# Recurrent pairs with all products as 64x64 quarters, in two row steps

## What is computed

```python
def wkv7_scan(r, w, k, v, kk, a, reverse):          # 8 heads of 64, per direction
    def step(state, inp):
        r_t, w_t, k_t, v_t, kk_t, a_t = inp
        sa = jnp.einsum('bhij,bhj->bhi', state, -kk_t)
        state = (state * w_t[:, :, None, :] + sa[..., None] * (kk_t * a_t)[:, :, None, :]
                 + v_t[..., None] * k_t[:, :, None, :])
        return state, jnp.einsum('bhij,bhj->bhi', state, r_t)
    ...
y = direction(0, False) + direction(1, True)
...
branch = jnp.einsum('bsnc,ncd->bsnd', ys, w_branch)  # three branches
gates = jax.nn.sigmoid(gl.reshape(b, s, N_BRANCH, D_MODEL) + b_gate)
merged = jnp.sum(gates * branch, axis=2)
```

## Time and profile before

| | |
|---|---|
| median of 3 runs | 2549.43 us (2548.84 to 2550.6) |
| the profiled execution | 2548.45 us |
| its span, first to last instruction | 2546.7 us |
| TensorE busy | 2484.2 us, 98% |
| VectorE, ScalarE, GpSimd busy | 1439.2, 527.6, 316.1 us |
| the pairs of layer 0, from the first scores to the mean (L972) | 194.96 to 353.67, 158.71 us |
| the pairs of layer 1 | 829.89 to 987.83, 157.94 us |

### The profile page before, as it was taken

The page is one execution under the profiler, slowest core; times in us unless marked ns, Lnnn a source line. Parts: engine busy times, 40 slices in busy tenths (PEclk is TensorE's granted clock), DMA queues, the critical chain, the costliest instruction groups (busy, mean ns, idle before and its releaser), DMA issues. The chain is left out here.

```text
span 2546.7 us, 38463 instructions
## 1 busy us (share of the span) xinstructions
PE 2484.2 (98%) x15968; PEld 1905.6 (75%) x15968; DVE 1439.2 (57%) x2688; ACT 527.6 (21%) x1249; POOL 316.1 (12%) x367
## 2 busy tenths in 40 slices
PE   8999999999999999999999999999999999999998
PEld 7887886854788788685477747888886666666997
DVE  1576655855157655573357735555334488854775
ACT  1342220100134222010014910000003243411000
POOL 2002102110100210221000000000000155410110
PEclk9999999999999999999999999999999999999999
DMA  7331125987433212598632022222222534334553
GB/s 269 116 116 63 57 81 170 303 292 256 147 116 117 68 52 84 179 306 289 239 125 67 2 66 71 96 83 75 91 87 69 165 101 135 121 102 146 167 173 107
DMA packets 253603, 341.80 MB, mean 134 GB/s; under 512 B 7252, under 2 KB 179412, under 8 KB 253304
## 3 DMA queue, kind: packets, MB, share of 16 engines
q1 hardware_dynamic: 241632, 311.71, 37.4%
q10 hardware_dynamic: 8920, 17.67, 2.1%
q0 software_dynamic: 2880, 9.96, 1.0%
HBM read 338.13 MB, written 1.19 MB: 133 GB/s over the span
## 5 line engine op out<-in xcount | busy, mean ns | idle before, releaser
L1058 PE MATMUL PS<-MEM 128*128 128x256 f32 (+1 forms) x2632 | 447.9, 332 | 2.6 <-ACT MEM L1515 1.2
L1058 PEld LDWEIGHTS PS<-MEM 128*128 128x128 f32 x2632 | 406.3, 190 | 43.8 <-issue 1.9
L416 PE MATMUL PS<-MEM 128*128 128x256 f32 x1632 | 356.0, 379 | 0.0
L1474 ACT ACTIVATE MEM<-PS 128x256 f32<-128x256 f32 (+4 forms) x405 | 162.0, 429 | 907.8 <-PE PS L416 221.1
L416 PEld LDWEIGHTS PS<-MEM 128*128 128x128 f32 x1632 | 308.6, 190 | 42.5 <-issue 1.3
L462 PE MATMUL PS<-MEM 128*128 128x512 f32 x608 | 265.4, 597 | 9.1 <-DMA MEM<-w_down 4.3
L2094 DVE SCALAR_TENSOR_TENSOR MEM<-MEM 128x512 f32<-128x512 f32 x280 | 214.4, 798 | 53.7 <-DMA MEM<-ada_w 48.0
L462 PEld LDWEIGHTS PS<-MEM 128*128 128x128 f32 x608 | 115.3, 191 | 155.3 <-issue 141.2
L3038 POOL TENSOR_TENSOR MEM<-MEM 128x1 f32<-128x1 f32 (+1 forms) x34 | 21.6, 637 | 1269.4 <-DVE MEM L2040 812.1
L696 PE MATMUL PS<-MEM 128*128 128x256 f32 x768 | 178.3, 384 | 0.0
L1371 PE MATMUL PS<-MEM 128*128 128x512 f32 (+1 forms) x512 | 171.5, 488 | 0.0
(11 more groups left out here) (384 smaller groups left out, 3259.8 us busy)
## 6 DMA issues: line engine op xcount, KB each, us to landing
MEM<-w_in SPq DMA_DIRECT2D x54, 1024.0 KB, 5.4
MEM<-ada_w SPq DMA_DIRECT2D x48, 1024.0 KB, 7.5
MEM<-w_up SPq DMA_DIRECT2D x32, 1024.0 KB, 5.4
MEM<-w_down SPq DMA_DIRECT2D x32, 1024.0 KB, 5.1
MEM<-ssm_w_in SPq DMA_DIRECT2D x24, 1024.0 KB, 5.4
MEM<-ffn_gate SPq DMA_DIRECT2D x22, 1024.0 KB, 5.3
MEM<-ffn_up SPq DMA_DIRECT2D x22, 1024.0 KB, 5.4
MEM<-ffn_down SPq DMA_DIRECT2D x20, 1024.0 KB, 5.1
```

What stands on the lines that cost most here:

```text
L416: ins = pe.matmul(bank[:, 0:T], W[:, k, c * P:(c + 1) * P], XT[:, k, :], start=k == 0, stop=k == KT - 1)
L1058: ins = pe.matmul(out, left[:, k, :], right[:, k, :], start=k == 0, stop=k == 3)
L1474: act.activation(out, view(b), func, **kw).then_inc(S("bank_read_by_act"), 1)
```

## The change

All products between the first scores and the end of the pairs become 64x64 quarters, apart from the transposes of the keys. Scores are split into two column halves. Two tiles are now summed together: in a first turn the upper 64 rows of one tile's contraction and the lower 64 of the other, each in two column halves, and in a second turn the other rows, behind a wait (`half_summed`) on the end of the first turn. One step is one contraction slice of both tiles in one turn, so a pair of tiles has as many steps as two tiles had. A slot ends when tiles end; steps left over are owed to the next slot. The slots' numbers are new.

Right side, solve and outputs take both groups of the pair together. Each is cut in two row steps: one with the 64 rows of each group that feed both column halves, the other with the rest, without the zero quarter; between them stands a wait (`row_step`) on the end of the first. The right side of both groups now has its first step after `level_xt` of level 3 and its second after `level_z` of level 4, and one bank per group instead of two. `solve_first` comes ahead of the slot XO, `solve_second` and `outputs_first` behind it, `outputs_second` and `outputs_third` behind the slot sa. ScalarE copies both right sides at level 4; VectorE reads the states of both groups ahead of the results.

```diff
--- before.py
+++ after.py
@@ -57,10 +57,10 @@
-FILL_SLOT = {"mask": (4, 0, 0, 0), "begin": (10, 0, 0, 0),
- ("z", 1): (2, 4, 4, 4), ("z", 2): (0, 0, 0, 0), ("z", 3): (0, 0, 0, 0), ("z", 4): (0, 0, 0, 0), ("z", 5): (4, 4, 4, 4),
- ("x", 1): (0, 0, 0, 0), ("x", 2): (0, 4, 4, 0), ("x", 3): (0, 0, 0, 0), ("x", 4): (0, 4, 4, 4), ("x", 5): (4, 4, 4, 4),
- "W": (4, 4, 4, 4), "XO": (2, 2, 2, 4), "sa": (2, 4, 4, 4)}
+FILL_SLOT = {"mask": (4, 0, 0, 0), "begin": (14, 0, 0, 0),
+ ("z", 1): (2, 2, 2, 2), ("z", 2): (0, 0, 2, 2), ("z", 3): (2, 2, 2, 2), ("z", 4): (2, 2, 2, 2), ("z", 5): (0, 2, 2, 4),
+ ("x", 1): (0, 0, 2, 0), ("x", 2): (0, 2, 2, 0), ("x", 3): (0, 0, 0, 2), ("x", 4): (0, 2, 2, 2), ("x", 5): (2, 2, 2, 4),
+ "W": (4, 4, 4, 4), "XO": (0, 2, 2, 4), "sa": (2, 4, 4, 4)}
@@ -427,7 +427,16 @@
-used = [0]
+used, halves, row_steps = [0], [0], [0]
+def rows_stepped(ins):
+    ins.then_inc(S("row_step"), 1)
+    row_steps[0] += 1
+def other_rows():
+    pe.wait_ge(S("row_step"), row_steps[0])
@@ -678,46 +687,61 @@
-    n_tiles = [0]
-    def open_tile(key):
-        n_tiles[0] += 1
-        return bank_for(key, None if spin[1] == NBANK else NBANK - 2 + n_tiles[0] % 2)
+    def pair_of_tiles(keys, by, W, c, src, nk):
+        if spin[1] == NBANK:
...
+            return
+        banks = [bank_for(key, NBANK - 2 + j) for j, key in enumerate(keys)]
+        for turn in range(2):
+            if turn:
+                pe.wait_ge(S("half_summed"), halves[0])
+            for k in range(nk):
+                for j, b in enumerate(banks):
+                    r = HB * (j ^ turn)
+                    for o in (0, HB):
+                        ins = pe.matmul(PS[o:o + HB, b, 0:T], W[r:r + HB, k, (c + j) * P + o:(c + j) * P + o + HB], src[r:r + HB, k, :],
+                                        start=turn == 0 and k == 0, stop=turn == 1 and k == nk - 1)
+                    if turn == 0 and k == nk - 1:
+                        ins.then_inc(S("half_summed"), 1)
+                        halves[0] += 1
+                    if turn == 1 and k == nk - 1:
+                        numbered(keys[j], by, b)
+                        done(ins)
+                if turn == 0 or k < nk - 1:
+                    yield 0
+        yield 2
     def gate_tiles(n):
         for s in range(4):
             W = a_slab(w_in[l], O_G + D * n + 256 * s)
-            for c in range(2):
...
+            work = pair_of_tiles([("gl", l, n, 2 * s + c) for c in range(2)], "act", W, 0, XT, KT)
+            yield from shut(work, 2)
     def branch_tiles(n, Y):
         for s in range(2):
             W = b_slab(w_branch[l, n], 0, 512 * s)
-            for c in range(4):
...
+            yield from pair_of_tiles([("br", l, n, 4 * s + c) for c in range(2)], "dve", W, 0, Y, 4)
+            work = pair_of_tiles([("br", l, n, 4 * s + c) for c in (2, 3)], "dve", W, 2, Y, 4)
+            yield from shut(work, 2)
+    def shut(work, tiles):
...
@@ -735,9 +759,16 @@
+    owed = [0]
     def slot(pair, name):
-        tiles_in[l, pair, name] = sum(next(gate_run) for _ in range(FILL_SLOT[name][pair]))
+        owed[0] += FILL_SLOT[name][pair]
+        tiles = 0
+        while owed[0] and not tiles:
+            tiles += next(gate_run)
+            owed[0] -= 1
+        tiles_in[l, pair, name] = tiles
@@ -784,7 +815,8 @@
             for half in range(2):
                 i, ct, pb, h = inst[2 * j + half]
                 rhs = KR[pb:pb + 64, d, ct, c, :, :].rearrange("p a b -> p (a b)")
-                ins = pe.matmul(banks[half][:, 256 * j:256 * j + 256], BK[pb:pb + 64, d, ct, c, part, :], rhs, start=True, stop=True)
+                for o in (0, HB):
+                    ins = pe.matmul(banks[half][o:o + HB, 256 * j:256 * j + 256], BK[pb:pb + 64, d, ct, c, part, o:o + HB], rhs, start=True, stop=True)
                 if j == 1:
                     done(ins)
@@ -871,55 +903,145 @@
                 if i == 3:
                     done(ins)
-    def right_side(g):
...
+    opened = {}
+    def open_banks(name, gs):
+        for g in gs:
+            opened[name, g] = bank_for((name, l, g))
+    def right_first(gs):
+        for g in gs:
+            emptied(pe, ("sk", l, g, 1))
+            if g >= 4:
+                emptied(pe, ("st", l, g - 4))
+        open_banks("rh", gs)
+        for i in range(4):
+            for g in gs:
+                d, c, wave, inst = instances(g)
+                _, ct, pb, h = inst[i]
+                f, b = HB * d, opened["rh", g]
+                to = [PS[o:o + HB, b, i * HB:(i + 1) * HB] for o in (0, HB)]
+                for j in range(2):
+                    ins = pe.matmul(to[j], AK[g % 2][f:f + HB, i, HB * j:HB * j + HB], VTK[f:f + HB, c, 64 * h:64 * h + 64],
+                                    start=i == 0, stop=wave == 0 and i == 3 and j == d)
...
+                if i == 3:
+                    rows_stepped(ins)
+    def right_second(gs):
+        other_rows()
+        for i in range(4):
+            for g in gs:
+                d, c, wave, inst = instances(g)
+                _, ct, pb, h = inst[i]
+                r, b = HB - HB * d, opened["rh", g]
+                to = [PS[o:o + HB, b, i * HB:(i + 1) * HB] for o in (0, HB)]
+                ins = pe.matmul(to[1 - d], AK[g % 2][r:r + HB, i, r:r + HB], VTK[r:r + HB, c, 64 * h:64 * h + 64],
+                                start=False, stop=i == 3 and (wave == 0 or pb != r))
...
+                if i == 3:
+                    numbered(("rh", l, g), "act", b)
                     done(ins)
-    def solve(g):
-        i2 = g % 2
-        emptied(pe, ("XO", l, g))
-        emptied(pe, ("rh", l, g, 1))
-        bank = take(("sa", l, g), "act")
+    def solve_first(gs):
+        for g in gs:
+            emptied(pe, ("rh", l, g))
+        open_banks("sa", gs)
         for i in range(4):
-            ins = pe.matmul(bank[:, i * 64:(i + 1) * 64], AB[g % 4][:, i, 0:P], RH[i2][:, i, :], start=True, stop=True)
...
+            for g in gs:
+                for o in (0, HB):
+                    ins = pe.matmul(PS[o:o + HB, opened["sa", g], i * HB:(i + 1) * HB], AB[g % 4][o:o + HB, i, o:o + HB], RH[g % 2][o:o + HB, i, :],
+                                    start=i == 0, stop=i == 3 and o == HB * (g % 2))
+                if i == 3:
+                    rows_stepped(ins)
+    def solve_second(gs):
+        for g in gs:
+            emptied(pe, ("XO", l, g))
+        other_rows()
+        for i in range(4):
+            for g in gs:
+                f = HB * (g % 2)
+                r, b = HB - f, opened["sa", g]
+                ins = pe.matmul(PS[r:r + HB, b, i * HB:(i + 1) * HB], AB[g % 4][f:f + HB, i, r:r + HB], RH[g % 2][f:f + HB, i, :],
+                                start=False, stop=i == 3)
+                if i == 3:
+                    numbered(("sa", l, g), "act", b)
+                    done(ins)
+    def outputs_first(gs):
...
+                to = PS[pb:pb + HB, opened["y", g], (i // 2) * P:(i // 2 + 1) * P]
+                pe.matmul(to, VTK[f:f + HB, c, 64 * h:64 * h + 64], AK[g % 2][f:f + HB, i, P:2 * P], start=i < 2, stop=False)
+                if wave and pb == f:
+                    pe.matmul(to, ST[pb:pb + 64, d, ct, :], KR[pb:pb + 64, d, ct, c, 1, :], start=False, stop=False)
+    def outputs_second(gs):
+        for g in gs:
+            emptied(pe, ("sa", l, g))
+        if gs[0] < 4:
+            open_banks("st", gs)
+        for i in range(4):
+            for g in gs:
+                d, c, wave, inst = instances(g)
+                _, ct, pb, h = inst[i]
+                f = HB * d
+                if wave == 0:
+                    to = PS[pb:pb + 64, opened["st", g], (i // 2) * 64:(i // 2) * 64 + 64]
+                    pe.matmul(to, BKT[g % 2][f:f + HB, 2 * (i // 2), pb:pb + 64], SA[g % 2][f:f + HB, i, :], start=i < 2, stop=False)
...
+                to = PS[pb:pb + HB, opened["y", g], (i // 2) * P:(i // 2 + 1) * P]
+                ins = pe.matmul(to, SA[g % 2][f:f + HB, i, :], AB[g % 4][f:f + HB, i, P:2 * P], start=False, stop=False)
+                if i == 3:
+                    rows_stepped(ins)
+    def outputs_third(gs):
+        other_rows()
...
+                ins = pe.matmul(PS[pb:pb + HB, b, o + r:o + r + HB], SA[g % 2][r:r + HB, i, :], AB[g % 4][r:r + HB, i, P + r:P + r + HB], start=False, stop=False)
+                ins = pe.matmul(PS[pb:pb + HB, b, o + r:o + r + HB], VTK[r:r + HB, c, 64 * h:64 * h + 64], AK[g % 2][r:r + HB, i, P + r:P + r + HB],
+                                start=False, stop=i >= 2 and not (wave and pb == r))
+                if wave and pb == r:
+                    ins = pe.matmul(PS[pb:pb + HB, b, o:o + P], ST[pb:pb + 64, d, ct, :], KR[pb:pb + 64, d, ct, c, 1, :], start=False, stop=i >= 2)
+                if i == 3:
+                    numbered(("y", l, g), "dve", b)
+                    done(ins)
     spin[:] = [0, NBANK - 2]
     for g in (0, 1):
@@ -936,8 +1058,8 @@
             if m == 2 and pair < 2:
```

(55 more changed lines are left out.)

94 lines of the change are left out of this document (45 added, 49 removed).

## The result

The changed kernel takes 2561.16 us (median of 4 runs, 2559.32 to 2563.61) for 2549.14 of the kernel before: 1.0047 times as long, 95% interval 1.0030 to 1.0065. The prediction was 2522.

A forecast was written before the change was run, and what follows sets the result against it. TensorE, busy 98% of the span, was taken as the bound. Per layer, work 122.2 + added waits 2.8 + front 3.8 + clock 1.6 + stalls 14.1 = 144.5 us, against 316.65 for both: 2522 median, 8-in-10 range 2497 to 2546.

The forecast's parts named there:

- Rival (1): Quarter passes over 256 columns don't run four quadrants at a time: 197 us per layer, 2626 us total; chance 0.07.
- The front: TensorE's idle time before the first level product of each layer's stage, 3.8 us per layer with 0.3 before the flips.
- chain: TensorE's stalls behind ScalarE's copies and VectorE's masks in the recurrent pairs: 14.1 us per layer, bounds half and double.
- Rival (2): Stalls on ScalarE and VectorE in the pairs take the whole gain back: 28 us instead of 14, total 2549; chance 0.10.
- Outputs: TensorE's work on the output products of the four pairs: 8.2 us per layer.
- levels: TensorE's work on the level products, 1856 passes at 14.9 ns: 27.7 us per layer.
- tiles: TensorE's work on the tiles, 960 quarter passes at 54.4 ns over 256 columns: 52.2 us per layer.
- rival (5): Instruction issue paces each quarter pass over 256 columns at 60 ns: 6.8 us more per layer, 2535 us; chance 0.01.
- The added waits: Also called own waits: half_summed and row_step waits in the stage, 7 x 0.4 = 2.8 us per layer.
- The clock: A stretch at granted clock 0.50 behind the idle time before the first level product: 1.6 us per layer.
- Drains: Time lost whenever TensorE leaves 64*64 passes for another split: 0.30 us each, about 48 per layer, some 14 us.
- Rival (4): Gaps between blocks come from waits, not the split, so 48 x 0.30 us stay: 2541 us; chance 0.05.

## Why the prediction was wrong

- **What held.** Quarters over 256 columns run four at a time: 32 passes from 195.75 to 197.48 in the kernel after, and 54.4 ns in the row measured alone. Rival (1) is out. The front came out at 4.1 for 3.8, with a stretch at 0.50 there, as said. The sum of work, own waits and chain was near, 139.1 for 141.7 and 139.0. Rival (2), the chain that takes it all back, is out as well: the chain's named waits are 3.2 us in layer 0, not 28.
- **That sum held by luck: two errors cancel.** The starts of consecutive passes in layer 0, less the waits that the trace names, add up to 142.1 us of work, 138.7 without the half-rate loss, where I had 122.2 and 2.8 of own waits. Outputs took 12.6 for 8.2, levels 33.2 for 27.7, tiles 59.8 for 52.2 (the half-rate time, mostly in the tiles, included). The paces were taken from blocks in full stream; that blocks which begin and end more often don't reach them is my reading, which no run tests. The chain's named waits were 3.2, where I had 12.6 without the branch tiles: the longer work and the stalls, as far as can be told, covered the rest.
- **The step that failed most**, by the trace's sums, is issue: the sum has no term for it, and rival (5), "Issue becomes the bound", got a chance of 0.01. Of the 16.7 and 20.6 us by which the stages exceed 144.5, the stalls without a releaser are 7.2 and 12.4. I priced issue as a pace per pass, and the trace did refuse that: 16 ns a pass runs. The limit is another: how fast the program arrives. 4209 passes for 2881 are 34 packets of instructions for 23 in each stage, and wherever 128 passes run in under some 3.5 us, TensorE stands for the rest. The 62 ns per matmul that the Trainium skill, "TensorE: Matmul & The Clock Gate", section "Wait — 56ns, not 53.3ns?", gives for one decode setting did not describe it: between the stalls passes over 64 columns run at 16 ns and passes over 256 columns at 54.4. (The prediction charged it to the passes over 256 columns alone; on the narrow ones it would have been far more.) The rows to see it by were in the trace of before, as the queue of instructions with its 16 KB packets, and as one wait of 0.35 us without a releaser; the prediction uses neither.
- **The added waits** are the other step that failed. I looked at the semaphores, between the turns of a pair and between row steps, priced those at 2.8, and missed that a pair takes both tile banks at once, so that a tile now waits for VectorE's reading of two: 4.8 and 3.5 us. I had only a neighbour of it, two branch tiles that reach VectorE in one slot of the last pair, 1.5. By the runs this step weighs most: with 14 of the 20 tiles whole, the waits of the tiles and at the front fall from 16.5 us in both layers to 1.6, the half-rate loss from 9.5 to 1.7, the stalls without a releaser only from 19.6 to 18.4, and the time goes from 2561 to 2543. No run takes these stalls away alone.
- **The clock** cost 3.4 and 6.1 us for 1.6: beyond the front, stretches at half rate stood at two waits of 0.92 and 1.32 us close together, at a stall of 1.60 without a releaser, and at one tile's wait of 1.86.
- **Drains.** That leaving 64*64 costs 0.30 us was neither shown nor refuted as such. Rival (4) was not needed: the run with whole tiles in small slots, which keeps these drains, is as fast as any here.
- **Outside the stages** 2.9 us were lost, 3.3 of them between the layers, where TensorE waits 1.6 us for w_up and 1.5 for w_down at once (before 0.5 at the most). I had written that nothing moves on SP's queue. No run took this apart; it stays open.

## What to carry to other kernels

Count TensorE's instructions before cutting products into smaller ones: here 128 passes need some 3.5 us to arrive, however short they are, so a long run of small products stands still between packets, and wants long ones beside it. When two results share the end of a step, ask who reads each bank and what that reader does first. And work that becomes shorter uncovers the waits it stood under; the same whole tiles went from 2557 to 2541 us when they were spread over the new gaps.

## What the runs showed of the hardware

- TensorE's program comes in packets of 16 KB, 256 instructions, while it runs. In the runs here 2.2 to 3.0 us lay between the start of a packet and the instruction that had waited for it, and in the stages two starts were never less than 3.2 us apart (3.35 in the kernel after).
- Where the borders of 256 fall is worth several us: the stage of layer 0 had 7.2 us of such stalls at one offset and 13.3 at another.
- Two waits in a row that are met already take one instruction: 368 of them add 184 to TensorE's trace. At the 72 and 112 instructions ahead of the stages TensorE stood 3.8 and 8.4 us.
